# Sixteen DRAM copies of a decoder step, cut into aligned runs of 15360 B

## What is computed

```python
ek = jnp.concatenate([buf_k, k_new.astype(buf_k.dtype)], axis=1)
ev = jnp.concatenate([buf_v, v_new.astype(buf_v.dtype)], axis=1)
...
return _combine_patterns(outs, lses).astype(q.dtype), ek[:, Sd:], ev[:, Sd:]
```

## Time and profile before

| | us |
|---|---|
| runs (three) | 1358.39 median, 1356.11 to 1365.81 |
| span of the profiled execution | 1348.5 |
| PE busy | 1191.7 (88%) |
| DVE, ACT, POOL busy | 487.8, 257.9, 240.1 |
| share of q1 (SP), q0 (POOL), q10 (ACT) in the 16 DMA engines' time | 67.1%, 19.4%, 6.5% |

### The profile page before, as it was taken

One profiled execution on the slowest core, in us unless ns is written; L12 is line 12 of the kernel. 1 busy time (PEld: TensorE's weight loads), 2 busy tenths in 40 slices (PEclk: granted clock), 3 DMA queues, 4 the chain that ended last, 5 costly groups with the idle time before them and its releaser, 6 DMA issues.

```text
span 1348.5 us, 17697 instructions
## 1 busy us (share of the span) xinstructions
PE 1191.7 (88%) x5864; PEld 610.3 (45%) x5864; DVE 487.8 (36%) x1388; ACT 257.9 (19%) x580; POOL 240.1 (18%) x281
## 2 busy tenths in 40 slices
PE   3999999967777878999899999999998998989981
PEld 1677785324342335445344444444443444444440
DVE  2356557024443442255623232232222222222344
ACT  2221111123332234021111111111111111111110
POOL 0200000023323220000012222121212122221220
PEclk9999999978888897999999999999999999999996
DMA  9989999999999997999599999999999999999844
GB/s 369 427 294 365 327 361 326 317 267 364 375 362 381 334 393 295 368 323 371 194 341 313 366 380 387 375 388 372 387 374 364 337 360 351 373 350 345 317 144 142
DMA packets 90942, 457.77 MB, mean 339 GB/s; under 512 B 15561, under 2 KB 17129, under 8 KB 73057
## 3 DMA queue, kind: packets, MB, share of 16 engines
q1 hardware_dynamic: 56960, 347.80, 67.1%
q0 software_dynamic: 28384, 80.50, 19.4%
q10 hardware_dynamic: 5504, 28.32, 6.5%
HBM read 435.20 MB, written 106.77 MB: 402 GB/s over the span
## 4 chain that ended last, share of the span: by engine, by line
PE 47%; DMA 35%; DVE 5%; issue 5%; SPq 3%; ACT 3%; ACTq 1%; POOLq 1%; POOL 0%; DVEq 0%
DMA routed_sum<-reg_w,sidx 28%; PE banks L741 9%; PE banks L1702 8%; PE banks L765 5%; PE banks L574 4%; PE banks L1692 4%; PE banks L636 2%; SPq L1536 2%; PE banks L1879 2%; DMA reg_w<-in_cache_v 1%; SPq L1537 1%; PE banks L1687 1%; DMA reg_s<-suffix_sums 1%; DMA reg_q<-in_cache_k 1%; PE banks L1837 1%
## 5 line engine op out<-in xcount | busy, mean ns | idle before, releaser
L741 PE MATMUL banks<-reg_q,reg_w 128*128 128x512 f32 (+1 forms) x624 | 233.6, 595 | 1.6 <-DVE reg_w L1136 1.6
L1459 POOL DMA_INDIRECT routed_sum<-reg_w,sidx x64 | 97.3, 1520 | 405.5 <-ACT reg_w L1323 255.0
L765 PE MATMUL banks<-reg_q,reg_w 128*128 128x512 f32 (+1 forms) x360 | 142.4, 609 | 8.2 <-ACT reg_w L1320 8.1
L741 PEld LDWEIGHTS banks<-reg_q,reg_w 128*128 128x128 f32 (+1 forms) x624 | 89.9, 167 | 126.6 <-issue 126.6
L741 PE MATMUL banks<-hT,reg_w 128*128 128x512 f32 (+1 forms) x208 | 91.9, 595 | 0.0
L1152 DVE SCALAR_TENSOR_TENSOR reg_w<-banks,small,reg_w 128x256 f32<-128x256 f32 x50 | 24.2, 484 | 183.4 <-ACT reg_w L1315 183.4
L1702 PE MATMUL banks<-hT,reg_q 128*128 128x260 f32 x384 | 87.9, 388 | 2.4 <-DVE hT L1963 1.6
L741 PE MATMUL banks<-reg_s,reg_w 128*128 128x512 f32 (+1 forms) x192 | 84.9, 595 | 0.0
L1702 PEld LDWEIGHTS banks<-hT,reg_q 128*128 128x128 f32 x384 | 73.8, 193 | 14.0 <-issue 2.6
L1455 POOL DMA_INDIRECT reg_w<-h_rows,gidx x50 | 52.6, 1051 | 154.1 <-DVE gidx L1101 138.1
L1968 DVE RECIPROCAL reg_s<-reg_s 128x520 f32<-128x520 f32 x16 | 54.4, 3398 | 65.4 <-ACT reg_s L2221 65.2
(11 more groups left out here) (374 smaller groups left out, 1512.1 us busy)
## 6 DMA issues: line engine op xcount, KB each, us to landing
reg_q<-in_w_gate_up SPq DMA_DIRECT2D x39, 2048.0 KB, 28.3
reg_q<-in_w_down SPq DMA_DIRECT2D x39, 1024.0 KB, 29.4
out_win_k_s<-in_win_k SPq DMA_DIRECT2D x8, 4094.0 KB
hT<-in_w_gate_up SPq DMA_DIRECT2D x13, 2048.0 KB, 28.6
reg_s<-in_w_gate_up SPq DMA_DIRECT2D x12, 2048.0 KB, 28.5
out_win_v_s<-in_win_v ACTq DMA_DIRECT2D x6, 4094.0 KB
reg_w<-in_w_ada SPq DMA_DIRECT2D x11, 2048.0 KB, 12.9
reg_w<-in_w_down SPq DMA_DIRECT2D x13, 1024.0 KB, 28.1
```

Source lines behind the costliest of these rows:

```text
L741: last = mm(pb[j % 2][of, :], lhsT=xT[:, j % 2, k, of], rhs=wgu[LOAD[p] % NBUF][:, k, :], start=(k == 0), stop=(k == KC - 1))
L765: last = mm(pb[6 + hh][of, :], lhsT=aT[:, j % 2, c, of], rhs=down_w(LOAD[p] % NBUF, c)[:, hh * 512:hh * 512 + 512], start=(c == 0), stop=( ...
L1459: nc.gpsimd.indirect_dma_start(rsum[n], bass.IndirectOffsetOnAxis(ap=idx[0:of.stop - of.start, :], axis=0), y[of, u, :], None, bounds_chec ...
```

## The change

Each of the 16 copies now takes 2040 of the 2047 rows, as 272 runs of 3840 floats (15360 B); run n begins at byte 15360 n, and as a row has 2 KB, source and destination of every run lie on multiples of 1 KB from their tensors' beginning. The other seven rows of every sample are copied by two more transfers, one for `win_k` and one for `win_v`, with 8 runs of 14336 B each. ACT issues both behind its last copy, after the fifth tile (t == QB). SP's last wait counts two more landings. When and by whom the 16 copies are issued is as before.

```diff
+MAIN, RUN = 2040, 3840
+assert MAIN * W % (16 * RUN) == 0
...
                     copy_window(act, n, win_out)
+                if t == QB:
+                    copy_window_ends(act, win_out)
...
-            sp.wait_ge(win_out, 16 * (2 * NS + TT))
+            sp.wait_ge(win_out, 16 * (2 * NS + 2 + TT))
...
             name, out, b = ("win_k", "win_k_s", n) if n < NS else ("win_v", "win_v_s", n - NS)
-            to, of = (t.rearrange("r c -> (r c)").rearrange("(x y n) -> y x n", x=2, n=PAST - 1)
-                      for t in (O[out][b, 0:PAST - 1, :], I[name][b, 1:PAST, :]))
+            to, of = (t.rearrange("r c -> (r c)").rearrange("(y n) -> y n", n=RUN)
+                      for t in (O[out][b, 0:MAIN, :], I[name][b, 1:MAIN + 1, :]))
             engine.dma_start(to, of).then_inc(done, 16)
+
+        def copy_window_ends(engine, done):
+
+            for name, out in (("win_k", "win_k_s"), ("win_v", "win_v_s")):
+                engine.dma_start(O[out][:, MAIN:PAST - 1, :].rearrange("b r c -> b (r c)"),
+                                 I[name][:, MAIN + 1:PAST, :].rearrange("b r c -> b (r c)")).then_inc(done, 16)
```

## The result

The changed kernel takes 1377.06 us (median of 4 runs, 1374.06 to 1378.01) against 1357.25 us before: 1.015 times, with a 95% interval of 1.0113 to 1.0187. It is 20 us slower, outside the range of the prediction. The profiled execution has a span of 1372.4 us where before had 1348.5. Span and run time of one execution differ by 1.7 us only (1374.06 us for the changed kernel's profiled one), so the trace of before belongs to an execution of about 1350 us, 7 us under the median of its runs: positions late in two traces can differ by some microseconds without a change of the kernel. (Lines from L134 on have other numbers in the changed kernel: L552, L574, L663, L741, L894, L1340 of before are L555, L577, L666, L744, L897, L1345.)

A forecast was written before the change was run, and what follows sets the result against it. PE was taken to set the pace in both copy stages, with a transfer mattering only where PE or its feeders wait, as at the suffix reads; 1358.4 - 1.4 + 3.6 gave 1360.6 us, range 1349 to 1372.

The forecast's parts named there:

- the six copies are hidden there: Second stage: the chain there consists of PE and small DVE and ACT steps, so ACT's six copies cost no time.
- 9.9 us above that span, which holds what lies around it: Whole kernel: the median of runs, 1358.39 us, lies 9.9 us above the profiled span of 1348.5 us.
- Step (1): First stage: aligned runs make copies 3% faster, 0.45 us each; the suffix reads' landing comes earlier, term -1.4 us.
- 288 GB/s in 226 to 238 us: First stage, copies alone: this rate becomes about 297 if right; under 266 means slower copies, over 340 much faster ones.
- the formula: End of SP's last copy: 0.5 us passed on from earlier copies plus 2 x 0.45 us, 1.4 us earlier.
- Step (2): Second stage: SP packets alternate with longer copy packets, ws_down lands 4.8 us later, PE waits; term +3.6 us.
- B: Whole kernel: nothing changes, a copy costs the same per byte and ws_down's load is not held; 1358 us, chance 0.20.
- Step (3): First stage: the eighth suffix read's issue holds ACT 2 or 3 us beyond 6.94, covered by PE's wait; counted as nothing.
- Step (4): Behind ACT's last copy: two short transfers delay the table load 1.2 us, covered by ACT's 3.40 us wait; nothing.
- C: First stage: other start addresses make copies alone slower; at 10%, +16.6 us in all, 1375 us; chance 0.12.
- A: First stage: copies alone near the rate of loads, gaining up to 9.0 us, turns costing little; 1349 us, chance 0.18.
- D: Whole kernel: faster by more than 1% through something outside the working; copies can give back 9.92 us idle; chance 0.04.

## Why the prediction was wrong

**What bounds the kernel, and where a copy can matter.** Right for the first stage: the wait at the suffix reads is the place, and SP's ten copies alone in the new cut gained 4.6 us there. Wrong for the second in what it left unsaid: "the six copies are hidden there" holds only while SP's loads keep their pace, and I named one of these, `ws_down`, but not the residual rows. In the trace of before the one issued at 563.61 us landed in 15.3 us and was used 2.4 us later (with packets of 15360 B it is the one that DVE waits 2.85 us for). Nothing in the prediction priced that cover: the loads of residual rows stood in it at nothing, without a reason given, and measured 38.1 us of waits of DVE. The price of a wait in lost clock was not in it either.

The prediction's "9.9 us above that span, which holds what lies around it" is a misreading that the sum does not hang on: 1.7 us lie around a span, and the rest is that the profiled execution was a quick one.

**Step (1), the rate.** The direction was right, the size too small: 3% taken, 1.4 us a copy measured (14.4 us over ten), about 10%, and 1.8 us in the stretch of copies alone. The sign that the prediction named, 288 GB/s in 226 to 238 us, can't be read as it stood: the changed kernel moves 218 there because the copies are done before the next is issued; over the busy part it is 338 for 295. What follows from it was wrong twice. The landing of the suffix reads was to come 1.4 us earlier, and with 1.4 us a copy the formula gives 0.5 + 2 x 1.4 = 3.3; it came 10.3 earlier (280.2 in the kernel with only SP's copies changed, 10.0 earlier). The last copy was done by about 268 us in place of 274 (in 268 to 274 us q1 moves 0.21 MB, 1.71 in before), and the reads behind it took less too; why that is more than two copies' savings is open. And the shift was counted "once, in full", while waits for cached keys took half of it back. That 3.3 is near the 4.6 us which SP's ten copies gained in the runs (1 to 8) is the luck of these two misses. The argument from the earlier trace rows, that the start address costs nothing since unaligned runs reach the full rate beside loads, was false: over the whole first stage, where copies mostly run alone, unaligned writes do cost, and a mixed stretch did not show it. The extra transaction (the Trainium skill, DMA: Bandwidth & Descriptors, How a descriptor splits into AXI transactions) is told there of the bytes before the start that are fetched, so of reads. Here reads 4 bytes off cost nothing, and writes 4 bytes off 0.8 us of 14.6, more than the 3% worked out from it.

**Step (2), the turns: the step that failed.** "Each SP packet will wait for a copy packet of 15360 B." The turns are there one for one, but the packet was 65280 B. I took its length from the diff and never asked whether 272 neighbouring runs stay 272; the rival that the change does not do what it says was put as "a copy costs the same per byte" (B) and not as runs that are joined. With packets of 15360 B the step's price of a turn came out, 665 ns where 649 were forecast, and the whole was within 1% of before (0.9988), as forecast for that change. PE L666 waited 4.07 us for `ws_down` where 3.6 were forecast, but in part by luck: the load took 2.3 us longer to land and not 4.8, was issued 0.6 us later, and PE was there 1.7 us sooner. Besides, the step counted the turns of one load and the store before it. It should have asked how many packets a tile of PE sends and how many turns a tile has room for: by the estimate above 16 x 0.87 us in 13.7 is the border, and beyond it each load waits for all before it.

**Step (3), the suffix reads.** The hold did not grow: the copy was gone sooner, the longest issue of a suffix read held ACT for 5.83 us in place of 6.94, DVE's wait fell to 3.8 us, and PE's steps before it did not come late. What a longer hold would have cost was not put to the proof.

**Step (4), the short transfers.** Right in the changed kernel. In order of time, ACT issues them, and its next ACTIVATE still waits 4.18 us for PE:

```profile
623.28 0.71 ACTq L1526 DMA_DIRECT2D out_win_k_s<-in_win_k  x1
624.01 0.67 ACTq L1526 DMA_DIRECT2D out_win_v_s<-in_win_v  x1
630.18 0.38 ACT L1265 ACTIVATE reg_w<-banks 128x256 f32<-128x256 f32 x1 [4.18 <-PE banks L639]
```

The hold of 14.04 us in the experiment with seven copies is more than this cover takes; the one of 9.64 us behind six copies of before was still covered.

**The rivals.** C named the time (1375 us) but not the way: its slower copies in the first stage did not come, they were faster. The range ended at 1372 because I saw slower copies as the only way to a loss. A was right in the first stage, whose landing came 10.3 us earlier where A allowed 9.0, and fell, with B, at the second. D was never near: without any copies the kernel is 9 us faster, inside the 9.92 us that D's bound went by.

## What to carry to other kernels

A run in an access pattern is not yet a packet: neighbouring runs listed in order of address are one piece and may be cut anew; count packets per queue in the trace (or bytes by packets) before believing a size. Where two queues share the DMA engines one for one, the short packets of one wait for the long ones of the other, so a transfer that nobody waits for belongs in short packets; compare packets an engine per step, times the turn, with the time of the step. Let each run of a DRAM write begin on a multiple of 64 B, which was as good here as any other start, where 4 bytes off cost 0.8 us a copy. A microsecond gained at one wait is not yet one gained at the end: ask which wait comes next. Look at what is queued behind a long transfer before making it longer.

## What was not expected of the hardware

- Of a DRAM to DRAM copy the start of the write counted and that of the read did not: with the same 61 MB, q1's share over 195 us is 86.6% aligned, 85.7% with the reads 4 bytes off, 90.6% with the writes 4 bytes off, 86.1% with both 64 bytes off (one trace each; two traces of one cut differ by less than 1 point).
- A packet of 65280 B is one turn: 127 of them for 128 packets of 4 KB in 23 us.
- An issue on ACT's queue can hold the engine: 14.04 us behind seven copies of 544 runs each, 2.98 us behind six of them, 0.71 us behind six copies of 64 packets.
